# Gates stage of a product-key expert kernel: fetched rows of U get three buffers in place of five

## The chip, the cores and the metric

One Trainium2 chip, one core of it. The metric is the device time of one execution in microseconds (us), the median of the runs of a kernel; lower is better.

## The reference, cut to what matters

One step of a decoder trunk: 1024 prompt tokens and 32 sample tokens, model width 1024, everything in float32. After the mixers each token goes through a layer of 16384 single-neuron experts, of which it uses 128 (8 heads, 16 each):

```
act = gelu(einsum('tkd,td->tk', expert_u[idx], x))     # 128 chosen rows of U a token
out = einsum('tk,tkd->td', gate * act, expert_v[idx])  # 128 chosen rows of V a token
```

The kernel splits the 1056 tokens. For 704 of them ("dense" tokens, TD) it computes the activations of all 16384 experts by matrix products with the whole of U, and uses the gates, zero where an expert was not chosen, as a dense matrix. For the other 352 (two tiles of 128 and one of 96, "sparse") it fetches the chosen rows of U and V from HBM one by one and does dot products and scaled adds.

## The kernel before

The stages in order are: the mixers (0 to about 640 us), the scores (to about 945 us), the choice of the experts (`peer_topk`, to 1442 us), the gates (`peer_gates`, to 2189 us), and the sum over V (`peer_down`, to the end). All are written out by hand: each engine has its own instruction list, and semaphores alone tie them together. There is a barrier between stages.

`peer_gates` does three things at once.

- **The upward products of the dense tokens.** 64 blocks of 128 experts are left (`UP_GATES`). For block n, SyncE loads a tile of U, 512 KB, into one of two buffers (`up.load`, L1782; tile `lead`). TensorE turns it (`up.turn`, L1803), ScalarE copies the turned tile (`up.high`, L1821), VectorE takes the low part (`up.low`, L1833), TensorE multiplies (`up.up`, L1813, 48 matmuls a block), ScalarE applies the gelu (L1828) and SyncE writes the result to HBM (`up.keep`, L1786).
- **The dense gate matrix.** It is built in 176 groups of four tokens. VectorE makes one-hot tiles for a group (L2344 and four times L2349, three buffers), TensorE multiplies them (L2384, eight instructions of the trace a group), ScalarE evicts them (L2404) into one of two large buffers (`room`, `pg_wb`), and when one is full, after 16 groups, SyncE writes it to HBM in four pieces of 1 MB during the next few groups (`write`, L2300). There are 11 such fillings, 44 pieces.
- **The rows of U of the sparse tokens.** The stage takes the last 256 columns of the choice (`NR`). For each, GpSimd issues one indirect DMA that brings 128 rows of 4 KB, 512 KB in all, into a buffer (`Rows.fetch`, L1852), and VectorE multiplies it with the tokens and sums (`Rows.dot`, L1861).

The work is laid out over 192 steps (`STEPS`), three a block. In a step VectorE first makes the groups due, then the low parts, then the dots due. A dot's place in VectorE's order is fixed, so that some steps have one dot and some have two one right behind the other. The buffers of the rows are a ring:

```
    def fetch(self, pool, i):
        if i >= self.n:
            pool.wait_ge(self.used, i - self.n + 1)
```

```
    def dot(self, dve, i, xs, raw):
        dve.wait_ge(self.fetched[i % self.n], 16 * (i // self.n + 1))
        ... .then_inc(self.used, 1)
```

So fetch i may be issued when dot i - n is done. n is the number of buffers: those given (here one, `lead.room[:, 2]`, which the trace shows as `lead`) and `more` own ones (`gr_row`). The stage before has n = 2 (`tk`: `lead` and `tr_row`), the stage after has n = 5. GpSimd has nothing else to do in the gates stage.

Of the kernel before, what the change touches and what calls it, by code (L numbers as in the profile page):

```python
# [1879 lines left out]
ROWS_TOPK = ROWS_A_TILE * (NT - 1)  # L1880
# [380 lines left out]
def peer_gates(nc, sel_t, w_d, u_d, up, lead, xs, idx, raw, lower):  # L2261


    with ExitStack() as ctx:
        def sb(name, shape, dt=F32):
            return ctx.enter_context(nc.sbuf_tensor("pg_" + name, shape, dt))
# [5 lines left out]
        NR = COLS - ROWS_TOPK  # L2272
# [4 lines left out]
        lower.place_first(nc)  # L2277

        wb = [lower.room[:].rearrange("p (i t) -> p i t", t=WCH), sb("wb1", [P, NK, WCH])]
        rows_u = Rows(ctx, nc, "gr", u_d, idx, ROWS_TOPK, NR, [lead.room[:, 2]], 4)  # L2280
        pw = [ctx.enter_context(nc.psum_tensor(f"pg_pw{b}", [P, BT, P], F32)) for b in range(2)]
        shaped, hot, made, stored = sem("shaped"), sem("hot"), sem("made"), sem("stored")
        wrote = [sem(f"wrote{b}") for b in range(2)]
# [428 lines left out]
def build(nc, A, O):  # L2712
# [9 lines left out]
    with nc.allow_non_contiguous_dma(reason="biases and S5 parameters, a few kilobytes"):  # L2722
# [3 lines left out]
        with ExitStack() as ctx:  # L2726
# [10 lines left out]
            with ExitStack() as c1:  # L2737
                xs = c1.enter_context(nc.sbuf_tensor("xs", [P, NXS, D], F32))
                h_d = [c1.enter_context(nc.sbuf_tensor(f"h_d{x}", [P, KD, TD], F32R)) for x in "hl"]
                sel_t = c1.enter_context(nc.sbuf_tensor("sel_t", [P, 3, TD], F32))  # L2740
                with ExitStack() as c2:
                    s_sb = c2.enter_context(nc.sbuf_tensor("s_sb", [P, NT, NU, NK], F32))
                    with ExitStack() as c3:
                        h_s = [c3.enter_context(nc.sbuf_tensor(f"h_s{x}", [P, KD, TSP], F32R)) for x in "hl"]
                        peer_scores(nc, lead, up, x2_order, ss2[:], A["peer_wq"][0], A["peer_keys"][0], h_d, h_s, xs,
                                    s_sb[:], sel_t[:], chosen[:].rearrange("p a c -> p (a c)"))
                    up.place(ctx, nc, h_d)
                    up.place_turns(turns, nc)
                    peer_topk(nc, s_sb, sel_t, u_d, up, lead, xs, idx, gate, raw)
                clear_sems(nc)  # L2750
                lower = Lower(ctx, nc, up, v_d, w_d, act_d)
                peer_gates(nc, sel_t, w_d, u_d, up, lead, xs, idx, raw, lower)
                turns.close()
# [28 lines left out]
```

## Time and profile before

| | before |
|---|---|
| median of 3 runs | 3256.96 us (3256.64 to 3259.86) |
| the profiled execution | 3260.44 us, of which the span from the first to the last instruction is 3258.7 |
| TensorE (matmul) busy | 3115.4 us, 96% of the span |
| VectorE busy | 2548.2 us, 78% |
| GpSimd busy | 1142.5 us, 35% |
| ScalarE busy | 875.4 us, 27% |
| DMA | 746.48 MB, mean 229 GB/s |

In the rows, PE is TensorE (PEld its weight loads), DVE VectorE, ACT ScalarE, POOL GpSimd, SPq the instruction queue of SyncE that issues DMAs. "busy" of a window is the time in which the engine had an instruction under way. PEclk is the TensorE clock that was granted, as a share of the full one. A bracket at the end of a row is the idle time of the engine ahead of this instruction and what ended it.

### The profile page before, as it was taken

The page shows a single profiled execution, that of the slowest core. Times are in us where ns is not written, and L with a number is a line of the kernel's source. Part 1 is how long each engine was busy: PE and PEld are TensorE (multiplying, and loading weights), DVE is VectorE, ACT ScalarE, POOL GpSimd, SP SyncE. Part 2 cuts the span into 40 slices and gives each one's busy share as a digit, 9 for nine tenths or more (in the row PEclk, how much of TensorE's full clock was granted, in tenths as well). Part 3 has the DMA queues.
Part 4 walks back from the last instruction along what each step waited for, and adds up shares of the span by engine and source line. Part 5 has one row for each costly group of instructions (what it writes and reads, how often), then busy time and mean ns, then how long its engine had stood idle before and what let it go on. Part 6 is the DMA issues. An engine that isn't in the chain of part 4 may idle for free. (4 is left out here: it accounts for less than half of the span.)

```text
span 3258.7 us, 45791 instructions
## 1 busy us (share of the span) xinstructions
PE 3115.4 (96%) x17420; PEld 2731.1 (84%) x17420; DVE 2548.2 (78%) x5671; ACT 875.4 (27%) x1294; POOL 1142.5 (35%) x757
## 2 busy tenths in 40 slices
PE   8999989899999999999999999998999999999998
PEld 7867755499999999999999999987777777777776
DVE  6611244332289999999989999867999999999996
ACT  4210300121122222234444444432222222222222
POOL 0000000000002212224434444333555886588881
PEclk9999989899999999999999999999999999999999
DMA  3010021321146666669889889899999999999993
GB/s 102 15 41 28 14 91 52 121 73 38 30 140 210 205 200 212 205 215 321 308 304 352 321 316 353 304 327 335 346 345 344 339 347 347 340 346 346 345 343 142
DMA packets 343266, 746.48 MB, mean 229 GB/s; under 512 B 36828, under 2 KB 189240, under 8 KB 337400
## 3 DMA queue, kind: packets, MB, share of 16 engines
q1 hardware_dynamic: 240472, 370.10, 32.9%
q0 software_dynamic: 102576, 373.47, 32.9%
q8 instruction: 138, 2.26, 0.3%
q14 instruction: 80, 0.66, 0.1%
HBM read 638.82 MB, written 102.25 MB: 227 GB/s over the span
## 5 line engine op out<-in xcount | busy, mean ns | idle before, releaser
L1852 POOL DMA_INDIRECT lead<-in_peer_v_dram,chosen x212 | 423.8, 1999 | 182.2 <-DVE acc_s L1871 129.8
L1852 POOL DMA_INDIRECT gr_row<-in_peer_u_dram,chosen x204 | 243.5, 1194 | 327.9 <-DVE chosen L1861 310.0
L1828 ACT ACTIVATE up_a<-up_pa 128x352 f32<-128x352 f32 x256 | 118.7, 464 | 760.5 <-PE up_pa L1813 688.8
L1852 POOL DMA_INDIRECT dr_row<-in_peer_v_dram,chosen x140 | 282.5, 2018 | 100.0 <-DVE acc_s L1871 72.5
L2581 DVE TENSOR_TENSOR acc<-pd_po,acc 128x512 f32<-128x512 f32 x384 | 268.1, 698 | 25.2 <-PE pd_po L2648 22.1
L1871 DVE SCALAR_TENSOR_TENSOR acc_s<-lead,chosen,acc_s 128x1024 f32<-128x1024 f32 x212 | 273.6, 1291 | 0.0
L2227 ACT ACTIVATE lo_wx<-room 128x704 fp32r<-128x704 f32 x128 | 101.5, 793 | 626.1 <-DVE room L2218 626.1
L1861 DVE CUSTOM_DVE_ANT_0 gr_row<-gr_row,xs 128x1024 f32<-128x1024 f32 x204 | 245.3, 1216 | 8.7 <-DMA gr_row<-in_peer_u_dram,chosen 8.6
L1852 POOL DMA_INDIRECT lead<-in_peer_u_dram,chosen x100 | 113.7, 1137 | 350.8 <-DVE chosen L1861 282.4
L511 PE MATMUL fr_a<-pj_w,h_t 128*128 128x256 f32 (+1 forms) x864 | 199.1, 393 | 0.9 <-PEq L186 0.9
L2349 DVE TENSOR_SCALAR pg_hot_i<-pg_iota,sel_t 128x128 f32<-128x128 f32 x704 | 195.2, 352 | 0.0
L511 PEld LDWEIGHTS fr_a<-pj_w,h_t 128*128 128x128 f32 (+1 forms) x864 | 170.7, 227 | 28.9 <-issue 6.9
L2384 PE MATMUL pg_pw<-pg_hot_i,pg_hot_j 128*128 128x128 f32 x1408 | 188.1, 277 | 2.0 <-DVE pg_hot_i L2349 2.0
L2384 PEld LDWEIGHTS pg_pw<-pg_hot_i,pg_hot_j 128*128 128x128 f32 x1408 | 178.8, 194 | 2.2 <-DVE pg_hot_i L2349 2.2
L1871 DVE SCALAR_TENSOR_TENSOR acc_s<-dr_row,chosen,acc_s 128x1024 f32<-128x1024 f32 x140 | 180.7, 1291 | 0.0
L1803 PE MATMUL up_pt<-up_ident,lead 128*128 128x128 f32 x1024 | 136.3, 277 | 26.9 <-DMA lead<-in_peer_u_dram 25.9
L2648 PE MATMUL pd_po<-up_ut2h,lo_wx 128*128 128x512 f32 x352 | 113.6, 397 | 35.8 <-issue 31.7
L2344 DVE TENSOR_TENSOR pg_hot_j<-pg_iota,sel_t 128x512 f32<-128x512 f32 x176 | 120.8, 686 | 31.8 <-PE pg_pw L2384 27.5
L1803 PEld LDWEIGHTS up_pt<-up_ident,lead 128*128 128x128 f32 x1024 | 119.8, 143 | 30.7 <-DMA lead<-in_peer_u_dram 28.2
L2648 PE MATMUL pd_po<-lo_vx4h,lo_wx 128*128 128x512 f32 x352 | 112.7, 394 | 25.0 <-issue 25.0
L1813 PE MATMUL up_pa<-h_dh,up_ut1h 128*128 128x352 f32 x688 | 132.9, 336 | 2.0 <-PEq L71 2.0
L1813 PE MATMUL up_pa<-h_dh,up_ut0h 128*128 128x352 f32 x688 | 129.8, 330 | 1.7 <-DVE up_ut0l L1833 1.7
(450 smaller groups left out, 7479.8 us busy)
## 6 DMA issues: line engine op xcount, KB each, us to landing
lead<-in_peer_u_dram SPq DMA_DIRECT2D x128, 512.0 KB
room<-in_peer_v_dram SPq DMA_DIRECT2D x128, 512.0 KB
act_d<-up_a SPq DMA_DIRECT2D x256, 176.0 KB
room<-w_d SPq DMA_DIRECT2D x64, 704.0 KB, 6.7
room<-act_d SPq DMA_DIRECT2D x64, 704.0 KB, 9.2
w_d<-pg_wb SPq DMA_DIRECT2D x24, 1024.0 KB, 8.6
w_d<-room SPq DMA_DIRECT2D x20, 1024.0 KB
pj_w<-in_w_in_dram SPq DMA_DIRECT2D x8, 1024.0 KB, 5.5
```

The costliest lines, as they stand in the source:

```text
L511: mm = nc.tensor.matmul(out, h_t[:, k, tok], w[piece % 2][:, k, :], start=(k == 0), stop=(k == KD - 1))
L1803: mm = self.nc.tensor.transpose(self.turn_bank(n, half)[:, k * P:(k + 1) * P], self.u_sb[n % 2][:, c:c + P], self.ident[:])
L1813: mm = self.nc.tensor.matmul(self.pa[c][:, 0:WB], self.ut[n % self.NB][x][:, k, :], self.h[y][:, k, c * WB:(c + 1) * WB], start=(i == 0), ...
L1828: self.nc.scalar.activation(self.a_sb[c][:], self.pa[c][:, 0:WB], ACT.Gelu_apprx_tanh).then_inc(self.a_act, 1)
L1852: pool.indirect_dma_start(self.buf[i % self.n], None, self.table, bass.IndirectOffsetOnAxis(ap=self.idx[:, col:col + 1], axis=0)).then_inc ...
L1861: self.nc.vector.tensor_tensor_reduce(row, row, xs[:, slot_of(col), :], 1.0, 0.0, ALU.mult, ALU.add, raw[:, col:col + 1]).then_inc(self.us ...
L1871: self.nc.vector.scalar_tensor_tensor(out=out, in0=self.buf[i % self.n], scalar=w[:, col:col + 1], in1=out, op0=ALU.mult, op1=ALU.add).the ...
L2344: nc.vector.tensor_tensor(hot_j[:, hb], iota[:].unsqueeze(1).broadcast_to([P, BT, P]), sel_t[:, 1, g * BT:(g + 1) * BT].unsqueeze(2).broad ...
L2349: ins = nc.vector.tensor_scalar(hot_i[:, hb, j, :], iota[:], sel_t[:, 0, tok], sel_t[:, 2, tok], ALU.is_equal, ALU.mult)
L2384: mm = nc.tensor.matmul(pw[g % 2][:, j, :], hot_j[:, g % NHB, j, :], hot_i[:, g % NHB, j, :], start=True, stop=True)
L2581: nc.vector.tensor_tensor(out, po[(OUTS * g + o) % NPO][:], out, ALU.add).then_inc(o_added, 1)
L2648: mm = nc.tensor.matmul(po[(OUTS * g + o) % NPO][:], lower.tokens(wx[g % 2][e], s, y), vx[g % 2][e][x][:, half * W4:(half + 1) * W4], star ...
```

## The change

The ring of row buffers of the gates stage has the given buffer and two own ones, three in all, where it had the given one and four. Nothing else is edited: the same 256 fetches, the same 256 dots, in the same places of the same instruction lists. What differs is the number in GpSimd's wait: fetch i waits for dot i - 3 where it waited for dot i - 5.

```
--- before.py
+++ after.py
@@ -2277,7 +2277,7 @@
         lower.place_first(nc)
 
         wb = [lower.room[:].rearrange("p (i t) -> p i t", t=WCH), sb("wb1", [P, NK, WCH])]
-        rows_u = Rows(ctx, nc, "gr", u_d, idx, ROWS_TOPK, NR, [lead.room[:, 2]], 4)
+        rows_u = Rows(ctx, nc, "gr", u_d, idx, ROWS_TOPK, NR, [lead.room[:, 2]], 2)
         pw = [ctx.enter_context(nc.psum_tensor(f"pg_pw{b}", [P, BT, P], F32)) for b in range(2)]
         shaped, hot, made, stored = sem("shaped"), sem("hot"), sem("made"), sem("stored")
         wrote = [sem(f"wrote{b}") for b in range(2)]
```

## Rows read from the trace of the kernel before

**Rows 1.** Windows: from, to, length, busy us by engine, PEclk, DMA share, GB/s.

```profile
1460.00:2060.00 600.00, 582.61 (x4113) 581.04 (x4113) 561.15 (x1304) 261.10 (x360) 250.24 (x209) 0.99 0.90 322
2060.00:2186.00 126.00, 118.24 (x783) 117.45 (x782) 89.43 (x187) 40.36 (x61) 46.70 (x39) 0.96 0.90 323
945.00:1440.00 495.00, 493.65 (x3206) 491.33 (x3205) 488.92 (x2022) 139.82 (x257) 101.79 (x96) 1.00 0.65 205
```

**Rows 2.** Waits of 1460 to 2060 us: in total, times, longest.

```profile
POOL gr_row L1852 <- DVE chosen L1861: 262.9, 127, 8.0
...
DVE pg_hot_j L2344 <- PE pg_pw L2384: 22.3, 34, 2.8
...
PEld up_pt L1803 <- DMA lead<-in_peer_u_dram: 18.9, 8, 4.2
...
DVE up_ut0l L1833 <- ACT up_ut0h L1821: 7.2, 3, 4.1
...
DVE up_ut1l L1833 <- ACT up_ut1h L1821: 2.6, 4, 1.1
DVE up_ut2l L1833 <- ACT up_ut2h L1821: 1.8, 2, 1.1
...
DVE gr_row L1861 <- DMA gr_row<-in_peer_u_dram,chosen: 1.2, 2, 0.7
```

**Rows 3.** Timeline, 1467 to 1479 us, a quiet stretch: dots and one fetch.

```profile
1467.88 1.21 DVE L1861 CUSTOM_DVE_ANT_0 gr_row<-gr_row,xs 128x1024 f32<-128x1024 f32 x1
...
1471.85 1.21 DVE L1861 CUSTOM_DVE_ANT_0 gr_row<-gr_row,xs 128x1024 f32<-128x1024 f32 x1
...
1473.34 1.15 POOL L1852 DMA_INDIRECT gr_row<-in_peer_u_dram,chosen  x1 [2.19 <-DVE chosen L1861]
...
1477.40 1.21 DVE L1861 CUSTOM_DVE_ANT_0 lead<-lead,xs 128x1024 f32<-128x1024 f32 x1
...
1478.54 1.21 DVE L1861 CUSTOM_DVE_ANT_0 gr_row<-gr_row,xs 128x1024 f32<-128x1024 f32 x1
```

**Rows 4.** Timeline: a fetch and its dot in the stage before; the start of this one.

```profile
1357.28 0.94 POOL L1852 DMA_INDIRECT lead<-in_peer_u_dram,chosen  x1 [5.31 <-DVE chosen L1861]
...
1362.63 1.22 DVE L1861 CUSTOM_DVE_ANT_0 lead<-lead,xs 128x1024 f32<-128x1024 f32 x1
...
1444.76 1.10 POOL L1852 DMA_INDIRECT lead<-in_peer_u_dram,chosen  x1 [0.44 <-issue]
...
1449.18 1.22 DVE L1861 CUSTOM_DVE_ANT_0 lead<-lead,xs 128x1024 f32<-128x1024 f32 x1 [3.12 <-DMA lead<-in_peer_u_dram,chosen]
...
1452.10 1.64 PE L2384 MATMUL pg_pw<-pg_hot_i,pg_hot_j 128*128 128x128 f32 x8 [1.99 <-DVE pg_hot_i L2349]
...
1457.21 1.22 DVE L1861 CUSTOM_DVE_ANT_0 gr_row<-gr_row,xs 128x1024 f32<-128x1024 f32 x1 [1.25 <-DMA gr_row<-in_peer_u_dram,chosen]
```

**Rows 5.** Timeline, two fetches in a loaded stretch, and below the dots that use them.

```profile
1518.78 1.15 POOL L1852 DMA_INDIRECT lead<-in_peer_u_dram,chosen  x1 [1.63 <-DVE chosen L1861]
1521.55 1.68 POOL L1852 DMA_INDIRECT gr_row<-in_peer_u_dram,chosen  x1 [1.62 <-DVE chosen L1861]
...
1531.46 1.22 DVE L1861 CUSTOM_DVE_ANT_0 lead<-lead,xs 128x1024 f32<-128x1024 f32 x1 [0.66 <-DMA lead<-in_peer_u_dram,chosen]
1532.61 0.08 DVE L1861 DVE_READ_ACCUMULATOR2_ANT chosen<- 128x1 f32 x1
1533.38 1.23 DVE L1861 CUSTOM_DVE_ANT_0 gr_row<-gr_row,xs 128x1024 f32<-128x1024 f32 x1 [0.69 <-DMA gr_row<-in_peer_u_dram,chosen]
```

**Rows 6.** Timeline, SyncE and then TensorE around one write of a filling.

```profile
1515.71 1.03 SPq L2300 DMA_DIRECT2D w_d<-pg_wb  x2
1520.10 0.32 SPq L1786 DMA_DIRECT2D act_d<-up_a  x1
1520.47 0.97 SPq L1782 DMA_DIRECT2D lead<-in_peer_u_dram  x1
1521.48 1.14 SPq L2300 DMA_DIRECT2D w_d<-pg_wb  x1
...
1534.94 1.97 PE L1803 MATMUL up_pt<-up_ident,lead 128*128 128x128 f32 x8 [3.26 <-DMA lead<-in_peer_u_dram]
```

**Rows 7.** Windows: quiet, with writes, and three behind a wait of TensorE.

```profile
1486.00:1506.00 20.00, 20.00 (x147) 20.00 (x146) 20.00 (x48) 10.07 (x14) 9.33 (x8) 1.00 0.86 275
1510.00:1530.00 20.00, 20.00 (x143) 20.00 (x142) 20.00 (x48) 8.90 (x13) 9.24 (x8) 1.00 0.97 376
1534.00:1538.00 4.00, 3.06 (x15) 3.06 (x16) 3.31 (x9) 1.19 (x2) 1.15 (x1) 0.57 1.02 412
...
1664.00:1671.00 7.00, 5.17 (x22) 5.17 (x23) 3.17 (x5) 3.10 (x4) 0.38 (x1) 0.52 0.73 292
2098.00:2104.00 6.00, 3.92 (x18) 3.92 (x19) 2.25 (x5) 2.46 (x5) 0.12 (x1) 0.50 0.80 290
```

**Rows 8.** Timeline, VectorE held by TensorE: all three one-hot buffers are full.

```profile
1547.84 0.69 DVE L2344 TENSOR_TENSOR pg_hot_j<-pg_iota,sel_t 128x512 f32<-128x512 f32 x1 [1.67 <-PE pg_pw L2384]
```

**Rows 9.** Timeline, the end of the stage.

```profile
2176.73 1.23 DVE L1861 CUSTOM_DVE_ANT_0 lead<-lead,xs 128x1024 f32<-128x1024 f32 x1 [1.18 <-DMA lead<-in_peer_u_dram,chosen]
...
2183.06 0.89 DVE L2218 TENSOR_TENSOR room<-room 128x704 f32<-128x704 f32 x1 [5.09 <-DMA room<-act_d]
...
2187.39 0.78 ACT L2227 ACTIVATE lo_wx<-room 128x704 fp32r<-128x704 f32 x1
```

More of the change, by code:

```diff
@@ L2279, in peer_gates @@
         wb = [lower.room[:].rearrange("p (i t) -> p i t", t=WCH), sb("wb1", [P, NK, WCH])]
-        rows_u = Rows(ctx, nc, "gr", u_d, idx, ROWS_TOPK, NR, [lead.room[:, 2]], 4)
+        rows_u = Rows(ctx, nc, "gr", u_d, idx, ROWS_TOPK, NR, [lead.room[:, 2]], 2)
         pw = [ctx.enter_context(nc.psum_tensor(f"pg_pw{b}", [P, BT, P], F32)) for b in range(2)]
```

## The prediction

> **What bounds the kernel now.** I read the windows first, stage by stage. The change acts in the gates stage alone, so the question is which engine sets that stage's pace and how far the others are behind. From 1460 to 2060 us TensorE is busy for 582.61 of 600 us [rows 1], and the list of waits gives the idle 17.4 us nearly whole to one cause: the tile of U that SyncE loads, 18.9 us in 8 waits by the row of the weight loads [rows 2]. TensorE sets the pace. VectorE is busy for 561.15 us, idle for 38.9, so it is a close second, 6.5% behind. Its idle time is mostly that it is too early: 22.3 us it waits until TensorE frees a one-hot buffer, 11.6 us it waits for turned tiles (7.2 + 2.6 + 1.8), and only 1.2 us for row buffers `gr_row` [rows 2]. GpSimd is held by the ring itself, 262.9 us in 127 waits for a dot [rows 2], and is no limit. The DMA engines are 0.90 busy at 322 GB/s [rows 1], which is near enough to full for the traffic to matter.
>
> The reader is to see two more things. When VectorE waits for a one-hot buffer [rows 8], three groups are made and not used up. The 176 groups are spread over 174 of the 192 steps of a stage of 745 us, 3.8 us a group, so VectorE then is two groups, some 8 us, ahead of TensorE. And the load is uneven: 275 GB/s in a quiet 20 us, 376 GB/s at a DMA share of 0.97 while a filled gate buffer is written [rows 7]. That happens 11 times in the stage, 9 times between 1460 and 2060 us.
>
> **The change part by part.** No instruction is added, removed or moved. What changes is the time that a fetch has. I cost four things.
>
> *1. The quiet stretches.* Fetch i now starts 0.28 us after dot i - 3 ends (the dot from 1471.85 ends at 1473.06, the fetch that it releases starts at 1473.34 [rows 3]). The tightest case is the second dot of a pair: the dot of 1478.54 has the one of 1471.85 as third before it [rows 3], so release to need is 1478.54 - 1473.06 = 5.5 us, less 0.28 leaves 5.2 us for the fetch. How long a fetch takes in quiet is bounded by two rows: 4.4 us from issue to dot, with the dot waiting (1444.76 to 1449.18), and at most 5.35 us without a wait (1357.28 to 1362.63) [rows 4]. So such a dot waits between 0 and 0.2 us in real quiet, and about 1 us where a fetch takes 6 us. There is a pair every 10.65 us (second dots at 1467.88 and 1478.54 [rows 3]), 56 in 600 us. The other dots have 6.7 us or more and don't wait. I take 0.35 us a pair, 20 us; bounds 0 and 56 x 0.9 = 50 us.
>
> *2. The stretches with writes.* There a fetch takes 12.7 and 11.8 us from issue to a dot that waits for it (1518.78 to 1531.46, 1521.55 to 1533.38) [rows 5]. With five buffers that is five rows on the way, so one lands every 2.4 to 2.5 us. Three on the way at the same rate need 7.3 us, and the ring turns round in 7.3 + 0.28 + 1.22 = 8.8 us, 2.9 us a row, against the 2.8 us at which VectorE wants them (255 intervals from 1449.18 to 2176.73 [rows 4, 9]). So the rate nearly holds. What is lost is the stock: two rows fewer lie ready when a write begins, 2 x 2.8 = 5.6 us. But these two rows, 1 MB, are then not moved at the expense of the write; at 376 GB/s [rows 7] that returns 2.8 us before the stretch is over. And some of the stock was never used: only 2 of the waits for `gr_row` fall in these 9 stretches [rows 2]. I take 2.3 us a stretch, 21 us; bounds 0 and 9 x 5.6 = 50 us.
>
> *3. What covers them.* The new waits stand in VectorE's order ahead of one-hots and low parts, and TensorE waits for those. The cover is VectorE's idle time, 38.9 less the 2 us in which it waits for rows already, and the 8 us that it is ahead [rows 8]: 45 us. Against it stand 20 + 21 = 41 us. If VectorE then led throughout, it would come through this stretch 4 us sooner than TensorE did, so nothing is left for the path: 0 us, bounds 0 and 100 - 45 = +55 us. At the start there is no such cover: TensorE waits for VectorE there (1.99 us), and the fourth dot already waits 1.25 us for its row [rows 4]. Its fetch and the next now start after a dot. I take +2 us, bounds 0 and 5.
>
> *4. What TensorE gets back.* The tile of U of 1520.47 was issued behind two writes of 1 MB and TensorE waited 3.26 us for it [rows 6]; behind such a wait its clock stands at the lower level of 1.2 GHz for a while (granted 0.57 in 1534 to 1538 us, 0.52 in 1664 to 1671, 0.50 in 2098 to 2104 [rows 7]), against 2.4 GHz else. With 1 MB less of rows ahead in the engines, such a tile can come up to 2.8 us sooner. Fully used that is most of the 18.9 us, and some 3 us of slow clock. But TensorE can use only what VectorE leaves, 4 us by step 3. From 2060 us on VectorE has 126 - 89.43 = 37 us idle [rows 1], and a little more can be had. I take -5 us in all, bounds -20 and 0.
>
> The end of the stage hides a late last row: behind the last dot (2176.73 + 1.23) VectorE idles 5.09 us for `act_d`, and ScalarE takes up its product only at 2187.39 [rows 9]. That is 8.5 us of cover, and past it each us would count in full.
>
> Sum: 0 + 2 - 5 = -3 us on the profiled execution's 3260.44, 3257.4. The median of the runs is 3.5 us below that execution, so 3254 us.
>
> The Trainium skill (DMA: Bandwidth & Descriptors, "Queues, rings and completion order") says that a DMA engine goes round between the queues that have work for it. By it three rows on the way would keep the share of five as long as the queue never runs dry, which agrees with the even 2.5 us of step 2, and a dry queue gives its turn to SyncE's loads, as step 4 has it.
>
> **The rivals.**
>
> *VectorE becomes the bound (slower).* Place: the second dots of pairs and the first dots behind a write. Price: what steps 1 and 2 sum to over 45 us. With 0.6 us a pair (34) and 3.5 us a stretch (31) it is 20 us over, and with the start 3257 + 22 = 3279; it decides once the new waits pass 45 us, that is 0.8 us on average for each of the 56 cycles of 10.65 us. For it: VectorE is only 6.5% behind and ran without a pause in both 20 us stretches of [rows 7]. Against it: the 2.4 us rhythm of landings, and its 8 us lead.
>
> *The loads of U gain much (faster).* Most of the 18.9 us goes, and in the last 126 us too. TensorE idles 7.8 us there [rows 1] with a clock of 0.96. That is 10 to 15 us: 3244. It needs new waits of VectorE under 30 us.
>
> *Nothing moves.* Quiet fetches come in 4.4 us, and rows and writes share the engines as before: 3257. The Trainium skill (DMA: Bandwidth & Descriptors, "Anatomy of one DMA") fits a DMA issued from GpSimd at 2.0 us and the bytes at 436 GB/s. By it a fetch would be an estimated 3.2 us and step 1 nothing; the trace's shortest here is 4.4 us [rows 4], so it is no more than a reason for this rival.
>
> **How the numbers follow.** A run can tell about 0.2% of this kernel, 6.5 us. The forecast has a chance of 0.40 (0.28 within 6.5 us, 0.09 faster, 0.03 slower), VectorE as the bound 0.30 (0.25 slower, 0.05 same), the gain of the loads 0.18 (0.13 faster, 0.05 same), nothing 0.12 (0.11 same, 0.01 slower). That gives faster 0.22, same 0.49, slower 0.29. The range reaches to the gain of the loads at 3243 and to VectorE as the bound at 3277; beyond lie the outer bounds of steps 1 and 2 (0.12) and of step 4 (0.05). The likeliest case alone has 3247 to 3262.
>
> **What would show it.** Waits of VectorE for `lead` and `gr_row` from 1460 to 2060 us grow from 2 us to 30 to 50 us, 0.3 to 0.4 us at second dots of pairs and 2 to 3 us behind writes. Its waits for TensorE and ScalarE fall from 34 us to under 10. TensorE's waits for the tile of U fall from 18.9 us to 10 to 15. The stage before and the stage after keep their lengths. I am wrong if TensorE gets many waits for `pg_hot_i` or for low parts (VectorE is the bound), or if a fetch in a loaded stretch still takes 11 us with three on the way (then a row costs 4 us there and step 2 is at its upper bound).

## The result, and the profile after

The kernel with three row buffers takes 3295.78 us (median of 4 runs, 3292.66 to 3298.48) against 3258.14 us before (4 runs): 37.6 us slower, ratio 1.0115 with a 95% interval of 1.0098 to 1.0133. The forecast was 3254 us with a range of 3243 to 3277. The rival "VectorE becomes the bound", which had 0.30, is what happened, and larger than it was priced (3279 us).

The windows of the kernel after, with the columns of [rows 1]: from 1460 to 2060 us, and the whole time in which the gate groups are made (from the first one-hot to the last).

```profile
1460.00:2060.00 600.00, 562.88 (x3894) 555.42 (x3892) 524.97 (x1217) 247.90 (x343) 231.07 (x196) 0.98 0.87 306
...
1445.00:2161.00 716.00, 673.36 (x4636) 664.98 (x4637) 629.04 (x1461) 293.65 (x405) 279.74 (x237) 0.98 0.87 303
```

The same time in the kernel before:

```profile
1444.00:2127.00 683.00, 657.71 (x4620) 655.74 (x4621) 627.92 (x1461) 293.32 (x405) 284.66 (x239) 0.99 0.89 319
```

This pair is the main reading. In a row, the first figure behind the length of the window is TensorE's busy time and the third is VectorE's. VectorE does the same work, 629.04 and 627.92 us with 1461 instructions, but in 716 us where it had 683. Its idle time goes from 55.1 to 87.0 us, and the stretch is 33 us longer. What the idle time consists of stands in the waits, first of the kernel after (1445 to 2161 us), then of the kernel before (1445 to 2126 us):

```profile
DVE gr_row L1861 <- DMA gr_row<-in_peer_u_dram,chosen: 54.9, 41, 4.1
...
PE pg_pw L2384 <- DVE pg_hot_i L2349: 40.7, 28, 3.6
DVE lead L1861 <- DMA lead<-in_peer_u_dram,chosen: 31.2, 22, 3.5
...
PE up_pt L1803 <- DMA lead<-in_peer_u_dram: 1.6, 1, 1.6
```

```profile
DVE pg_hot_j L2344 <- PE pg_pw L2384: 27.5, 40, 2.8
PE up_pt L1803 <- DMA lead<-in_peer_u_dram: 23.1, 9, 5.7
...
DVE lead L1861 <- DMA lead<-in_peer_u_dram,chosen: 5.7, 3, 3.1
DVE gr_row L1861 <- DMA gr_row<-in_peer_u_dram,chosen: 3.0, 4, 1.2
...
PE pg_pw L2384 <- DVE pg_hot_i L2349: 2.0, 1, 2.0
```

The roles are exchanged. Before, VectorE waited for TensorE (27.5 us for a free one-hot buffer) and TensorE for its tile of U (23.1). After, VectorE waits for nothing but rows, 54.9 + 31.2 = 86.1 us against 8.7, and TensorE waits for VectorE's one-hots, 40.7 us against 2.0. Its waits for the tile of U are down to 1.6 us. That seems to be mostly because it asks later: the loads themselves landed little sooner, 9.7 us after their issue beside a write (median of 21) where it had been 10.5 us (median of 22).

That count, and the others below that speak of landings, is made from the semaphore updates with which a transfer reports that it has landed, which the traces hold beside the rows. A fetch or load counts as beside a write when it was under way within 7 us of the issue of one.

The rows of a loaded stretch after, GpSimd's fetches and then the dots that use them:

```profile
1510.17 1.15 POOL L1852 DMA_INDIRECT lead<-in_peer_u_dram,chosen  x1 [1.63 <-DVE chosen L1861]
...
1521.66 1.15 POOL L1852 DMA_INDIRECT lead<-in_peer_u_dram,chosen  x1 [5.79 <-DVE chosen L1861]
1524.43 1.15 POOL L1852 DMA_INDIRECT gr_row<-in_peer_u_dram,chosen  x1 [1.63 <-DVE chosen L1861]
```

```profile
1520.15 1.23 DVE L1861 CUSTOM_DVE_ANT_0 lead<-lead,xs 128x1024 f32<-128x1024 f32 x1 [3.50 <-DMA lead<-in_peer_u_dram,chosen]
...
1530.27 1.23 DVE L1861 CUSTOM_DVE_ANT_0 lead<-lead,xs 128x1024 f32<-128x1024 f32 x1 [3.33 <-DMA lead<-in_peer_u_dram,chosen]
...
1535.46 1.23 DVE L1861 CUSTOM_DVE_ANT_0 gr_row<-gr_row,xs 128x1024 f32<-128x1024 f32 x1 [1.12 <-DMA gr_row<-in_peer_u_dram,chosen]
```

With at most three rows on the way a fetch still takes 10.0, 8.6 and 11.0 us from issue to the waiting dot, not the 7.3 us of step 2. With five buffers it was 12.7 and 11.8 [rows 5]. These are the fetches that were waited for. Of all that were issued from 1460 to 2060 us beside a write, the median from issue to landing is 9.0 us with three buffers (64 fetches) and 9.9 us with five (76); in quiet it is 5.6 and 5.8 us. So two buffers fewer shorten a fetch by 1 us.

The end of the stage after, VectorE and then TensorE:

```profile
2220.99 1.23 DVE L1861 CUSTOM_DVE_ANT_0 lead<-lead,xs 128x1024 f32<-128x1024 f32 x1 [0.41 <-DMA lead<-in_peer_u_dram,chosen]
...
2222.14 0.89 DVE L2218 TENSOR_TENSOR room<-room 128x704 f32<-128x704 f32 x1
```

```profile
2212.03 1.43 PE L1813 MATMUL up_pa<-h_dh,up_ut1l 128*128 128x352 f32 x8
2225.51 0.77 PE L2648 MATMUL pd_po<-up_ut2h,lo_wx 128*128 128x512 f32 x1 [12.04 <-PEq L2264]
```

Before, the last dot was done 5.09 us before the product of L2218 could begin [rows 9], and TensorE stood still for 4.05 us between the stages:

```profile
2190.09 0.77 PE L2648 MATMUL pd_po<-up_ut2h,lo_wx 128*128 128x512 f32 x1 [4.05 <-PEq L2264]
```

Now the last dot ends at 2222.2, the product follows at once, and TensorE stands still for 12.04 us. The last dot is what holds the product back: the load of `act_d` that the product also needs had landed at 2213.8. The account of the span, 3291.8 - 3258.7 = 33.1 us: 1 us ahead of the stage; 33.0 while the groups are made (the last one-hot ends at 2126.6 before, 2160.5 after); -6.5 from there to the last upward product (2186.0 and 2213.5); 8.0 between the stages; -2.3 in the stage after. Of the -6.5 us, 2.4 are VectorE's lost lead (TensorE finished its last group 5.6 us behind the last one-hot before, 3.2 us after), 2.1 are a wait for a tile of U that is gone, and the rest goes with the clock behind that wait (granted 0.97 in this stretch before, 1.00 after). The median moved by 4.5 us more than the span of these two executions.

### The profile page after: what moved, and what is told of

It is laid out like the page before. It is cut to its first block and busy times, and to the rows that moved or that the text cites. A ratio compares the mean times of both kernels' runs of the same rounds, so it can differ in the third digit from the quotient of the medians.

```text
span 3291.8 us, 45791 instructions
## 1 busy us (share of the span) xinstructions
PE 3130.6 (95%) x17420; PEld 2739.1 (83%) x17420; DVE 2549.9 (77%) x5671; ACT 872.9 (27%) x1294; POOL 1136.9 (35%) x757
## 5 line engine op out<-in xcount | busy, mean ns | idle before, releaser
L1852 POOL DMA_INDIRECT gr_row<-in_peer_u_dram,chosen x170 | 198.6, 1168 | 317.7 <-DVE chosen L1861 301.7
L1852 POOL DMA_INDIRECT lead<-in_peer_u_dram,chosen x134 | 153.0, 1142 | 409.1 <-DVE chosen L1861 340.0
L1861 DVE CUSTOM_DVE_ANT_0 gr_row<-gr_row,xs 128x1024 f32<-128x1024 f32 x170 | 207.0, 1222 | 78.7 <-DMA gr_row<-in_peer_u_dram,chosen 78.0
L2384 PE MATMUL pg_pw<-pg_hot_i,pg_hot_j 128*128 128x128 f32 x1408 | 193.4, 282 | 40.8 <-DVE pg_hot_i L2349 40.7
L1861 DVE CUSTOM_DVE_ANT_0 lead<-lead,xs 128x1024 f32<-128x1024 f32 x134 | 163.5, 1220 | 35.5 <-DMA lead<-in_peer_u_dram,chosen 35.1
L1813 PE MATMUL up_pa<-h_dh,up_ut2h 128*128 128x352 f32 x672 | 131.8, 340 | 0.4 <-DVE up_ut2l L1833 0.4
```

What stands on the lines that cost most here:

```text
L1813: mm = self.nc.tensor.matmul(self.pa[c][:, 0:WB], self.ut[n % self.NB][x][:, k, :], self.h[y][:, k, c * WB:(c + 1) * WB], start=(i == 0), ...
L1852: pool.indirect_dma_start(self.buf[i % self.n], None, self.table, bass.IndirectOffsetOnAxis(ap=self.idx[:, col:col + 1], axis=0)).then_inc ...
L1861: self.nc.vector.tensor_tensor_reduce(row, row, xs[:, slot_of(col), :], 1.0, 0.0, ALU.mult, ALU.add, raw[:, col:col + 1]).then_inc(self.us ...
L2384: mm = nc.tensor.matmul(pw[g % 2][:, j, :], hot_j[:, g % NHB, j, :], hot_i[:, g % NHB, j, :], start=True, stop=True)
```

## The experiments

All are compared by their medians with the kernel before on the same chip, which gave 3256.8 to 3257.4 us. The kernel with three buffers was measured once, with the result above; differences to its 3295.78 us go across chips and are less sharp. "Waits for rows" is the sum of VectorE's two rows of the kind shown above, up to its last one-hot.

No edit touches anything ahead of the gates stage, and yet that stage starts at 1437.2 us in one profiled execution and at 1447.6 in another. So the length of the stage, from the first one-hot to the first product of the stage after, says more on an edit than the span of a profiled execution. It is known to some 5 us at best: with four buffers it is 5.2 us shorter than with five, at the same median.

| kernel | median us | stage us |
|---|---|---|
| before, five buffers | 3258.14 | 745.7 |
| after, three buffers | 3295.78 | 780.2 |
| four buffers | 3257.23 | 740.5 |
| three, small writes | 3230.95 | 719.8 |
| five, small writes | 3218.23 | 709.3 |
| three, writes spread out | 3309.38 | 791.6 |
| three, finer writes | 3280.78 | 775.0 |
| five, finer writes | 3282.82 | 769.4 |
| three, even dots | 3276.62 | 765.0 |
| three, even dots, finer writes | 3269.99 | 759.0 |
| five, load of U first | 3232.28 | 716.5 |
| four, load of U first | 3233.44 | 721.0 |
| three, load of U first | 3296.22 | 780.9 |
| four, even dots, load of U first | 3235.92 | 725.8 |

### Four buffers

```
-        rows_u = Rows(ctx, nc, "gr", u_d, idx, ROWS_TOPK, NR, [lead.room[:, 2]], 4)
+        rows_u = Rows(ctx, nc, "gr", u_d, idx, ROWS_TOPK, NR, [lead.room[:, 2]], 3)
```

> Four row buffers. Theory A (in a stretch with writes the rows land at a fixed low rate however many are on the way, and only rows that already lie ready cover it): VectorE waits for rows 30 to 45 us from 1445 us to its last one-hot, against 86 with three and 9 with five; that stays under its 56 us of idle time, so 3258 to 3268 us. Theory B (a fetch of normal length does not fit the 5.2 us at the second dot of a pair): the window becomes 8 us, the waits vanish, 3256 to 3260 us. Theory C (any buffer less costs in proportion): half of the 37.6 us, 3277 us.

Measured: 3257.23 us, ratio 1.0001 (0.9990 to 1.0013). The waits, 1445 to 2126 us:

```profile
DVE gr_row L1861 <- DMA gr_row<-in_peer_u_dram,chosen: 21.6, 25, 2.6
...
DVE pg_hot_j L2344 <- PE pg_pw L2384: 15.9, 23, 1.9
DVE lead L1861 <- DMA lead<-in_peer_u_dram,chosen: 8.3, 5, 3.2
```

There are new waits, 29.9 us against 8.7, and they cost nothing: VectorE's wait for TensorE falls from 27.5 to 15.9 us. This is what the cover of step 3 says, and against theory B, by which no waits would be left, and theory C, by which half the loss would show. Both figures lie just below what theory A had named (30 to 45 us of waits, 3258 to 3268 us).

### Three and five buffers with small writes

```
-                own = slice(piece * NK // PIECES, (piece + 1) * NK // PIECES)
+                own = slice(piece * NK // PIECES, piece * NK // PIECES + 4)
...
-        sp.dma_start(self.w[r % 2], self.w_d[:, :, m:m + 2, :]).then_inc(self.w_in[r % 2], 16)
+        sp.dma_start(self.w[r % 2], self.w_from[:, :, m:m + 2, :]).then_inc(self.w_in[r % 2], 16)
```

Each of the 44 writes carries 128 KB in place of 1 MB, so seven eighths of the gates never reach HBM. `w_from` is a view of V in HBM of the same shape, which the stage after reads in place of the gates.

> Three row buffers, each of the 44 writes of gates cut from 1 MB to 128 KB, and the stage after reads the gates from another tensor of the same shape in HBM (part of V), so that the output isn't the reference's. To be compared with the same cut at five buffers. Theory A: the loaded waits (77 us) vanish, 35 to 45 us of waits in quiet remain and are covered by VectorE's idle time, so at most 5 us over five buffers with the cut. Theory B: 60 us or more of waits remain and the kernel is 20 to 35 us over the one with five buffers.

> Five row buffers with the same cut of the writes. Both theories: no waits for rows behind the first, no waits of TensorE for the tile of U (25 us before), no slow clock behind them: 3220 to 3240 us.

Measured: 3230.95 us with three, 3218.23 us with five, 12.7 us apart where whole writes give 37.6. The waits with three, 1445 to 2096 us, where its last one-hot is:

```profile
DVE gr_row L1861 <- DMA gr_row<-in_peer_u_dram,chosen: 14.5, 24, 1.8
DVE lead L1861 <- DMA lead<-in_peer_u_dram,chosen: 13.0, 13, 2.2
PE pg_pw L2386 <- DVE pg_hot_i L2351: 4.3, 7, 2.1
```

27.5 us of waits are left of 86.1, and TensorE waits 4.3 us for one-hots. Some of the waits stand at the second dots of pairs, as in the first two rows, and some at other dots, as in the rest:

```profile
1706.03 1.23 DVE L1861 CUSTOM_DVE_ANT_0 gr_row<-gr_row,xs 128x1024 f32<-128x1024 f32 x1
1707.80 1.23 DVE L1861 CUSTOM_DVE_ANT_0 lead<-lead,xs 128x1024 f32<-128x1024 f32 x1 [0.54 <-DMA lead<-in_peer_u_dram,chosen]
...
1895.29 1.23 DVE L1861 CUSTOM_DVE_ANT_0 gr_row<-gr_row,xs 128x1024 f32<-128x1024 f32 x1
...
1896.49 1.23 DVE L1861 CUSTOM_DVE_ANT_0 lead<-lead,xs 128x1024 f32<-128x1024 f32 x1
...
1899.27 1.22 DVE L1861 CUSTOM_DVE_ANT_0 gr_row<-gr_row,xs 128x1024 f32<-128x1024 f32 x1
...
1903.51 1.23 DVE L1861 CUSTOM_DVE_ANT_0 gr_row<-gr_row,xs 128x1024 f32<-128x1024 f32 x1 [1.38 <-DMA gr_row<-in_peer_u_dram,chosen]
```

The dot of 1903.51 has the pair among the three before it, so its fetch too had only 5.3 us from its release to the moment at which VectorE was free for it. I call this time the window. Counted over 1460 to 2060 us, 11 of 25 us of waits stand at second dots and 14 at others.

So two thirds of the waits come from the writes, which theory A says and theory B does not. The size was off: 35 to 45 us of waits were to be left, and the time was to be 5 us over five buffers at most. Of the 12.7 us, the two profiled executions show 10.5 in the stage: 7.2 while the groups are made (658.1 and 650.9 us) and 5.4 between the stages (8.1 and 2.7 us), less 2.1 from the last one-hot to the last upward product.

### Three buffers, writes spread out

```
-                    if c >= 0 and b < PIECES:
+                    if c >= 0 and b % 4 == 0:
...
-                        write(c, b)
+                        write(c, b // 4)
```

> Three row buffers, all writes whole, but the four pieces of a filling are issued four groups (15 us) apart instead of one group (3.8 us). Theory A: one piece at a time is over in about 6 us and costs one late row, so the waits fall from 86 us to 45 to 65 and the time to 3258 to 3275 us. Theory B: the waits at second dots of pairs stay, 3285 to 3300 us.

Measured: 3309.38 us, 13.6 us slower than three buffers with the writes in a row. The waits, 1445 to 2167 us:

```profile
DVE gr_row L1861 <- DMA gr_row<-in_peer_u_dram,chosen: 68.9, 45, 4.7
...
DVE lead L1861 <- DMA lead<-in_peer_u_dram,chosen: 26.8, 19, 3.3
```

95.7 us instead of 86.1. Theory A in this form falls. I had thought of a filling as one long stretch that uses up the stock of ready rows, so that pieces apart would be harmless. The landings say why they are not: beside a single piece a fetch still takes 7.1 us in the median, where the shortest windows have 5.2 us. And from 1460 to 2060 us 134 fetches are now beside a write, where with the pieces in a row it was 64, at 9.0 us in the median.

### Finer writes, with three and with five buffers

```
+SUB = 4
...
-                sp.dma_start(w_d[:, c, own].rearrange("j i t -> j (i t)"),
...
+                for q in range(SUB):
+                    part = slice(own.start + q * NK // PIECES // SUB, own.start + (q + 1) * NK // PIECES // SUB)
+                    sp.dma_start(w_d[:, c, part].rearrange("j i t -> j (i t)"),
```

The counts in the waits for these writes grow with them.

> Three row buffers; each 1 MB piece of a write goes out as four DMAs of 256 KB at once, with runs of 2 KB a partition instead of 8 KB. The same bytes at the same places. Theory T (rows and writes take turns by descriptors, so a row is held by the long descriptors of a write): rows get four times the share beside a write, the loaded waits fall from 77 us to under 40, 3262 to 3275 us. Theory W (the bytes alone count: a 1 MB write holds the row on its way by the time its bytes take): loaded waits stay at 65 to 85 us, 3288 to 3302 us.

> Five row buffers with the same fine writes. Theory T: rows win against writes, so filled buffers go out later and TensorE's waits for the tile of U (behind them in SyncE's queue) grow: 3257 to 3270 us. Theory W: as before the change, 3253 to 3262 us.

Measured: 3280.78 us with three (15.0 us faster than three with whole pieces by the medians, 5.2 us by the stage of the profiled executions) and 3282.82 us with five (ratio 1.0071, 1.0052 to 1.0090, to the kernel before). Five buffers, 1445 to 2150 us:

```profile
PE up_pt L1803 <- DMA lead<-in_peer_u_dram: 35.8, 12, 6.5
...
DVE lead L1861 <- DMA lead<-in_peer_u_dram,chosen: 3.3, 1, 3.3
...
DVE gr_row L1861 <- DMA gr_row<-in_peer_u_dram,chosen: 0.9, 1, 0.9
```

Two things change. The rows come sooner: beside a write a fetch lands after 8.0 us where it took 9.9 at five buffers, and after 7.7 where it took 9.0 at three, and the waits for rows are 4.2 us against 8.7 and 76.0 against 86.1. That is theory T in its direction, but at three buffers the waits were to halve. And TensorE waits 35.8 us for tiles of U against 23.1. For this the edit brings a cause of its own, which no theory named. Each DMA, short or long, keeps SyncE's queue for half a microsecond, and there are four times as many:

```profile
1653.79 4.35 SPq L2303 DMA_DIRECT2D w_d<-pg_wb  x8
1658.18 1.85 SPq L1786 DMA_DIRECT2D act_d<-up_a  x1
1660.08 1.62 SPq L1782 DMA_DIRECT2D lead<-in_peer_u_dram  x1
```

Eight DMAs, two pieces, took 4.35 us, where two whole pieces took 1.03 us [rows 6], and the load behind them was issued late. In the kernel before, all ten loads that TensorE had to wait for were issued 10.3 us behind the end of the turn that freed their buffer. With finer writes there are twelve, and eleven of them were issued 0.3 to 2.8 us later than that. Once issued, a load beside a write lands after 10.7 us, as before (10.5). So the tiles come later because they are issued later; that they lose turns to the rows is not seen. Theory W, by which nothing would change, falls.

### Even dots

```
+                first = 4 * (s // 3) + (0, 2, 3)[s % 3]
+                if s < STEPS:
+                    rows_u.dot(dve, first, xs, raw)
                 if s >= 2 and k == 1 and n + 2 < NK:
                     up.low(dve, n + 2, 0)
                     up.low(dve, n + 2, 1)
-                if s < STEPS:
-                    for i in range(NR * s // (STEPS - 2), min(NR, NR * (s + 1) // (STEPS - 2))):
-                        rows_u.dot(dve, i, xs, raw)
+                if s < STEPS and s % 3 == 0:
+                    rows_u.dot(dve, first + 1, xs, raw)
```

> Three row buffers, the 256 dots laid out evenly: four in every block of three steps, the two of the first step with the two low parts between them, so that no dot stands right behind another. The window from release to need is then at least 6.5 us everywhere instead of 5.2. If the quiet waits (36 us) come from the pairs they fall under 10 us, all waits to 45 to 65 us, and the time to 3257 to 3272 us. If the windows of three buffers are too short everywhere, the waits stay over 75 us and the time over 3285 us.

> Three row buffers, even dots and fine writes. Theory T: waits under 30 us, all covered, 3252 to 3262 us. Theory W: as the even dots alone, within 4 us.

Measured: 3276.62 us for the even dots, 19.2 us faster than three buffers as they were; 3269.99 us with the fine writes too. The waits of the even dots, 1445 to 2138 us:

```profile
DVE gr_row L1861 <- DMA gr_row<-in_peer_u_dram,chosen: 46.6, 33, 4.3
PE pg_pw L2386 <- DVE pg_hot_i L2349: 23.1, 14, 4.5
DVE lead L1861 <- DMA lead<-in_peer_u_dram,chosen: 21.7, 17, 3.2
```

68.3 us of waits against 86.1 (17.8 less). With the fine writes too they are 50.4 us, where under 30 were expected. Of the 58.8 us from 1460 to 2060 us in the run with whole pieces, 53.8 stand at dots whose fetch was under way beside a write. The waits are over the cover, so TensorE still waits 23.1 us for one-hots. Both runs end above their ranges (3272 and 3262 us): the last dots now stand two steps later, and TensorE stands still for 16.8 and 14.6 us between the stages.

### The load of U first

Two lines of SyncE's list swapped, with five, four and three buffers, and with four and even dots:

```
                 if k == 1:
-                    up.keep(sp, n, 0)
                     if n + 3 < NK:
                         up.load(sp, n + 3)
+                    up.keep(sp, n, 0)
```

> Five row buffers, and SyncE issues the load of the next tile of U before it waits for the half activation that it writes out (two lines swapped), some 5 us sooner. If TensorE with its waits for that tile (25 us and the slow clock behind them) is what bounds the stage at five buffers, most of them go: 3225 to 3245 us. If VectorE is as near as its idle time says (56 us up to the last one-hot), it does not take the gain back.

> Four row buffers with the early load. At four buffers VectorE waits for rows for about 37 us of its 56 us of idle time. If that cover is the right account, a gain of TensorE of 25 us is more than the 19 us that are left: 3234 to 3250 us, slower than five with the early load. If not, the same as five.

> Three row buffers with the early load. TensorE waited only 1.8 us for the tile of U here and VectorE sets the pace with 86 us of waits for rows: no gain, 3288 to 3302 us. If a gain over 15 us shows, TensorE still had part in the pace at three buffers.

> Four row buffers, even dots and the early load. The even dots add 1 us to the shortest window. With the waits for rows under 30 us VectorE keeps up: 3228 to 3245 us; the last dots end a step later, which can cost up to 5 us at the end of the stage.

| | median us | ratio to before, 95% |
|---|---|---|
| five buffers | 3232.28 | 0.9923 (0.9905 to 0.9942) |
| four buffers | 3233.44 | 0.9926 (0.9903 to 0.9949) |
| four, even dots | 3235.92 | 0.9936 (0.9917 to 0.9956) |
| three buffers | 3296.22 | 1.0122 (1.0103 to 1.0142) |

The waits with five, 1445 to 2126 us, and the window of 1460 to 2060:

```profile
DVE pg_hot_j L2344 <- PE pg_pw L2384: 8.5, 16, 2.7
DVE gr_row L1861 <- DMA gr_row<-in_peer_u_dram,chosen: 7.6, 7, 1.5
...
PE up_pt L1803 <- DMA lead<-in_peer_u_dram: 3.0, 4, 1.0
```

```profile
1460.00:2060.00 600.00, 597.73 (x4259) 596.97 (x4258) 577.15 (x1346) 266.91 (x372) 262.27 (x216) 1.00 0.91 334
```

With five and four buffers TensorE's waits for the tile all but go (3.0 and 2.8 us), it is busy for 597.73 of 600 us with five, and 24 to 25 us are won. With three nothing is won: the waits for the tile were at 1.6 us already, and the time is that of three buffers without the edit (3295.78). That shows which engine sets the pace on either side. Four buffers were expected to be slower than five; by their medians they are level within the intervals (by the stage 4.5 us slower), so VectorE may have had a little more room than the account gave it.

## Why the prediction was wrong

**Which engine bounds the kernel before, and how near the second is.** Right. TensorE with its waits for the tile of U set the pace; the swapped lines, which take these waits away, win 25 us at five buffers.

**Step 1, quiet stretches.** Near in size, and partly by luck. It took 20 us in 600, bounds 0 and 50. With small writes 25 us of waits were left in 600, but only 11 of them at second dots of pairs. That "the other dots have 6.7 us or more and don't wait" was a wrong reading: in the kernel before, from 1460 to 2060 us, 31 of the 156 other dots had a window of 5.2 to 5.5 us, and only 19 of the 54 second dots. The two errors about cancel. The fetch in quiet was also longer than taken, 5.6 us in the median of the kernel after where the bounds were 4.4 and 5.35.

**Step 2, stretches with writes.** This is the step that failed. In 1460 to 2060 us VectorE waits 74.4 us for rows (49.3 for `gr_row`, 25.1 for `lead`); less the 25 that small writes leave, the nine stretches have 49 us, 5.5 each, where I took 2.3 and the bound was 5.6. Counted dot by dot in the kernel after, 61 of the 74.4 us stand at dots whose fetch was under way beside a write, 6.8 a stretch, which is past the bound. The second count is the higher one because it also takes in waits that would stand there without the write.

What failed is "three on the way at the same rate need 7.3 us". It divided the time of a fetch by the number on the way and took the quotient for a rate. Neither figure held. The kernel before did not have five rows on the way: when the two fetches of [rows 5] were issued it had four, themselves counted, and over the 600 us 2.6 on average, because a buffer whose row has landed early lies full until its dot. And the rows did not land every 2.4 to 2.5 us: between the landings of 1520.78 and 1531.44 there are three intervals of 3.6 us on average, slower than VectorE wants them. The kernel before lived on its stock there. Among its own fetches beside a write, those issued as the third on the way took 8.8 us in the median, those issued as the fourth 10.8. So the kernel before itself gives about 9 us for a fetch with three on the way, and the kernel after shows it, 9.0 in the median and 8.6 to 11.0 where VectorE waited. Given such fetches the sum leaves no room for the 2.8 us that were to be "returned before the stretch is over". The spread writes show why the picture of a stock was not apt for three buffers: single pieces cost at least as much as four in a row. The prediction named the sign by which this would be seen, a fetch that still takes 11 us with three on the way, and it was seen.

**Step 3, the cover.** Right as a rule and as a size for VectorE's order. Four buffers put 29.9 us of waits into it at no cost; at three buffers the account closes, 86.1 us of waits for rows and 1.6 at the start against 55 us of idle time before, 33 us over. The 8 us of lead in the cover were too many for this stretch: they show only behind the last one-hot, and as 2.4 us. Only the sum that was held against it was too small, 41 instead of 74 us in the 600. At the start the fourth dot waited 0.54 us where it had waited 1.25, so the 2 us that I gave it did not come.

**Step 4, TensorE's gain.** The waits for the tile fell from 25 to under 2 us, further than forecast, but mostly, it seems, because TensorE came later: beside writes the loads landed 0.8 us sooner in the median, not 2.8. Nothing of it was won while the groups were made, where VectorE set the pace. Behind the last one-hot some 4 us were, a wait of 2.1 us and the slow clock behind it.

**The end of the stage.** I gave it 8.5 us of cover. The last dot came 8.7 us after the last upward product instead of 8.1 before it, and 8.0 us stand on the path between the stages. The rival had left this out too: where it had 22 us, there are 33 us of the groups and 8.0 here, less 6.5 and 2.3, which is 32, and 1 us ahead of the stage.

What stays open is how the DMA engines share their time between a write and the rows. The length of the runs matters for the rows (8.0 us for a fetch beside finer writes where it took 9.9). The Trainium skill (DMA: Bandwidth & Descriptors, "Queues, rings and completion order") says that a DMA engine takes turns between its queues by packets; the shorter fetches agree with it, if shorter runs make shorter turns, which no run here shows by itself. But the finer writes removed 10 of about 59 us of waits only. Whether a short row queue loses turns when it runs dry was not measured by itself.

## What to carry to other kernels

A prefetch ring's depth is to be judged in the stretch where the transfers are slowest, with the time of a fetch as it is there and not divided by the number on the way. The window is (buffers x interval) less the use, on average 3 x 2.8 - 1.2 = 7.2 us here, but where two dots stand close together it was 5.2 us, and the dots behind a pair count as well as its second dot. Against that stood 5.6 us in quiet and 9 to 11 us beside writes. Sum the shortfall and hold it against the idle time of the engine that waits; up to that sum buffers can be taken away for nothing (four for five here), beyond it every us counts, and the end of the stage, where the last transfer stands on the path, counts by itself. Before the buffers, look at the order in one queue: a load that stood behind a wait it did not need was worth 25 us for two swapped lines. And count the DMAs that stand ahead of it: each took its queue 0.5 us here, at 256 KB as at 1 MB.

## What the runs showed of the hardware

- A gather of 128 rows of 4 KB took 4.4 us from issue to its waiting dot at the start of the stage [rows 4]. Beside writes of 1 MB it took 11.8 and 12.7 us where VectorE waited for it with five buffers and 8.6 to 11.0 us with three; in the median of all such fetches 9.9 and 9.0 us. It does not fall in proportion to the number of buffers.
- A 1 MB write as four of 256 KB with runs of 2 KB instead of 8 KB let the fetches beside it land sooner (9.9 to 8.0 us at five buffers) and took 10.1 us off the waits for rows at three (86.1 to 76.0). It kept the issuing queue for about 2 us in place of 0.5, 0.5 us a DMA at either size, and TensorE's waits for the tiles issued behind it grew by 12.7 us (23.1 to 35.8).
- The write traffic of the gates costs 39 us in all at five buffers (3257.32 to 3218.23 us). With the writes left whole, issuing the load of U earlier won 25 us.
